# GpSimd in place of VectorE for the sums that rebuild a block of h

## The chip, the cores and the metric

The kernel runs on one core of one Trainium2 chip, in one launch, in fp32. The metric is the device time of a run in microseconds (us). The engines are TensorE (PE; its weight loads are PEld), VectorE (DVE), ScalarE (ACT), GpSimd (POOL) and SyncE (SP), which issues most of the DMAs. Each engine works through its own list of instructions in order, and they wait for each other by semaphores.

## The reference, cut to what matters

Two layers over 512 latent and 256 context tokens of width 1024. Each layer is a half feed-forward block, a token mixer, and another half feed-forward block, each modulated by adaLN and followed by a layer norm. The part that the change touches is the feed-forward block:

```python
def half_ffn(x, shift, scale, gate, w_in, w_out, g, b):
    h = modulate(x, shift, scale)
    a, u = jnp.split(h @ w_in, 2, axis=-1)
    y = (jax.nn.silu(a) * u) @ w_out
    return layernorm(ALPHA * x + 0.5 * gate * y, g, b)
```

It runs four times. Three of these calls are over all 768 tokens (`ffn0`, `ffn1` and `ffn2`, the "wide" ones); the last one, `ffn3`, is over the latent tokens alone and is built by other code.

## The kernel before, in words

**Precision.** Each fp32 operand of a product is split into a high part (a copy rounded to the matmul format fp32r) and a low part (the operand less its high part). A product is three matmuls: high by high, high by low, low by high. `HHI` and `HLO` hold the parts of h, 8 chunks of 128 rows by 768 tokens.

**Seven products.** A wide feed-forward block has 11 iterations (`FI`), each for two slots, A and B, of 128 columns of the gate half and of the value half. From iteration 2 on, the product of h with these columns is done by a seven-product scheme (`up`, L3153) on blocks of h: half of the rows by half of the tokens (`HALF` is 384). Four blocks are mixtures, kept as high parts `TH_` and low parts `TL_` (numbers 1, 2 and 3, each as two tiles k of 2 chunks by 384 tokens); the fourth mixture overwrites a quarter of h itself, the first four chunks over the last 384 tokens. The seven products of a slot come in this order: "11", "T2", "21", "T3", "T1", "T4", "22"; each is 12 matmuls of 384 columns. The semaphore `g_pe` counts the first five, `pe[slot]` the last two. Between them VectorE adds the results up in `P1`, `U3` and `GM` (`second_sum`, `gate_first`, `third_sum`, `fourth_sum`, `up_second`, `up_first`, `gate_second`), ScalarE applies silu to each half of `GM`, and VectorE multiplies (`gated_first`, `gated_second`).

**The last iteration** (L2326 to L2356 on VectorE, L3241 to L3245 on TensorE). Slot A goes through the seven products, then TensorE does the 16 groups of the previous iteration's second product (`down`, L3191), and slot B is done in the plain way (`up_classic` with `rebuilt`, L3094). `rebuilt` needs the quarter of h that was overwritten. So while the last slot A is in work, VectorE rebuilds it, for each k: `rebuild_mix(k)` sums high and low of block "11" and both parts of block 1 in the tile `TM_[2][k]`, three sums of 128x768 elements, each of which waits for the one before; `rebuild_parts(k)` splits that tile in `TH_[2][k]` (a copy) and `TL_[2][k]` (a difference). `TM_[2]` lies in the same bytes as `TL_[2]`, so it waits until product "T2" of this slot is done (`g_pe` at 5 * first + 2). `rebuild_mix(0)` stands between `gate_first` and `third_sum`; `rebuild_parts(0)` after `up_second`; `rebuild_mix(1)` between `gated_first` and `gate_second`; `rebuild_parts(1)` after the first four `accumulate`. In `ffn0` and `ffn1`, `tables()` (14 and 21 tiny VectorE instructions on coefficients) stands after `rebuild_parts(0)`.

**Banks.** `accumulate(i, e)` (L2043) adds the result e of `down` to X and so frees its PSUM bank. TensorE's groups e = 0 to 3 need no bank freed; group 4 waits until `accumulate` 0 is done (L3208).

**Other lines that are spoken of.** `split_lo` (L1719) makes the low part of a 128x1024 slab of weights, after ScalarE has made its high part (L1059). GpSimd (L802 on) issues the loads of the adaLN weights and makes partial sums for the layer norms (`add_chunks`, L838, first needed when X gets its last results); in the odd mixer it makes low parts too (L925, L959). L1837 centers X for a layer norm, L2267 adds the last results to X, L2771 scales a softmax row in the odd mixer.

Of the kernel before, what the change touches and what calls it, by code (L numbers as in the profile page):

```python
# [24 lines left out]
HALF = TOK // 2  # L25
# [6 lines left out]
FI = FC // 2  # L32
# [6 lines left out]
F32 = mybir.dt.float32  # L39
F32R = mybir.dt.float32r  # L40
ACT = mybir.ActivationFunctionType
ALU = mybir.AluOpType
# [105 lines left out]
def build(nc, A, out):  # L148
    stack = ExitStack()

    def sem(name):
        return nc.alloc_semaphore(name)
# [4 lines left out]
    def sb(name, shape, dt=F32, at=None):  # L157
        size = 4 * int(np.prod(shape[1:]))
        if at is None:
            at = free[0]  # L160
            free[0] += -(-size // 32) * 32
        assert at + size <= 229344, (name, at + size - 229344)
        return nc.alloc_sbuf_tensor_at(name, list(shape), dt, offset=at)
# [4 lines left out]
    HHI = sb("HHI", [P, KC, TOK], F32R)  # L168
    HLO = sb("HLO", [P, KC, TOK], F32R)
# [37 lines left out]
    def region(start, end):  # L207
# [3 lines left out]
        def place(name, shape, dt=F32):  # L211
# [13 lines left out]
    TH_ = {n: [place(f"TH{n}{k}", [P, 2, HALF], F32R) for k in range(2)] for n in (1, 2)}  # L225
    TL_ = {n: [place(f"TL{n}{k}", [P, 2, HALF], F32R) for k in range(2)] for n in (1, 2)}
    TL_[3] = [place("TL30", [P, 2, HALF], F32R)]
    TM_ = {n: [sb(f"TM{n}{k}", [P, 2, HALF], F32, at=r2 + 17408 + 3072 * (4 + 2 * (n - 1) + k)) for k in range(2)]
           for n in (1, 2)}
# [147 lines left out]
    s_pe, s_max, s_nb, s_exp, s_inv, s_norm, t_pe, pt_hi, pt_lo, av_pe, o_tmp, o_add = (  # L377
        sem(n) for n in ("s_pe", "s_max", "s_nb", "s_exp", "s_inv", "s_norm", "t_pe", "pt_hi", "pt_lo", "av_pe", "o_tmp", "o_add"))
    g_hi, g_lo, g_mix, g_pe, g_p1, g_add = (sem(f"seven_{n}") for n in ("hi", "lo", "mix", "pe", "p1", "add"))
    t_mix, t_hi, t_lo = (sem(f"t_{n}") for n in ("mix", "hi", "lo"))  # L380
    och_hi, och_lo = sem("och_hi"), sem("och_lo")
    fin_x, fin_tr, fin_cp = sem("fin_x"), sem("fin_tr"), sem("fin_cp")
    h_hi, h_lo = sem("h_hi"), sem("h_lo")
# [5 lines left out]
    count = dict(q=0, A=0, B=0, W=0, evac=0, g=0, gB=0, gs=0, ln=0, h=0, tr=0, ada=0, taken=0)  # L389
# [42 lines left out]
    def raw_slot(q):  # L432
        return q % 2
# [77 lines left out]
    BLOCKS = {"ffn0": 0, "ffn1": 1, "ffn2": 2}  # L511

    def wide_q(name, kind, i):

        q = plan[name].q
        if isinstance(i, int) and i == 0:
            return q + {"B": 2, "A": 4, "W0": 6}[kind]
        if isinstance(i, int) and i == FI - 1:
            return q + 6 * i + {"W1": 1, "B": 2, "W0": 4, "W1L": 5}[kind] - 6 * i
        return q + {"B": 1, "W1": 3, "A": 4, "W0": 6}[kind]  # L520

    def seven(name, slot, i):

        return UNITS * BLOCKS[name] + 2 * (i - 2) + "AB".index(slot)
# [21 lines left out]
    def last_evac(name, S, a, m):  # L546

        return plan[name].evac + KC * S * (FI - 1) + KC * a + m + 1
# [14 lines left out]
    def part(name, a):  # L563

        if name in HALVED:
            return CTX * a, CTX, 0
        s = ORDER[LN_PARTS[name]][a]
        return *SEGS[s], s
# [234 lines left out]
    def _(pool):  # L803
# [9 lines left out]
        def ada_loads(l, n0, group, i=0):  # L813

            for k in range(KC):
                slot = k % ADA_RING
                if not (isinstance(i, int) and KC * (n0 + i) + k < ADA_RING):

                    pool.wait_ge(ada_used, KC * n0 + k - ADA_RING + 1 + KC * i)
                src = A["ada_w"][l, k * P:(k + 1) * P, :].rearrange("p (g n) -> p g n", n=D)[  # L820
                    :, bass.ds(group, 1), :].squeeze(1)
                pool.dma_start(ADA[slot][:, :], src).then_inc(ada_in[slot], 16)  # L822
# [7 lines left out]
        def add_chunks(name, S, a, evicted):  # L830

            lo, n, _ = part(name, a)
            total, (count, done) = RSTD[:, lo:lo + n], adds(name, a)
            for m in range(1, count + 1):
                pool.wait_ge(evac, evicted(a, m))
                if m > 1:
                    pool.wait_ge(ln_add, done + m - 1)
                pool.tensor_tensor(total, X[:, 0, lo:lo + n] if m == 1 else total, X[:, m, lo:lo + n],  # L838
                                   ALU.add).then_inc(ln_add, 1)

        def last_sums(name, prev):

            evicted = lambda a, m: last_evac(prev, 2, a, m)
            add_chunks(name, 2, 0, evicted)
            add_chunks(name, 2, 1, evicted)

        last_sums("ln0", "ffn0")
        pool.wait_ge(evac, plan["ln0"].evac)
        for n in range(3):
# [19 lines left out]
        pool.wait_ge(evac, plan["ln1"].evac)  # L869
        with pool.Fori(0, N_ADA) as i:  # L870
            ada_loads(1, plan["ffn1"].ada, i, i)
        last_sums("ln2", "ffn1")
        last_sums("ln3", "ffn2")


# [117 lines left out]
    def _(act):  # L993
# [123 lines left out]
        def wide(name, ada, nxt):  # L1117
            p = plan[name]
            blk = BLOCKS[name]
# [80 lines left out]
                unit("B", i, lambda: rows_hi(1, wide_q(name, "W1", i), i, p.W + 2 * KC * (i - 1)), wide_q(name, "A", i))  # L1200

            def t_high(dst, src, count):
                act.wait_ge(t_mix, 28 * blk + count)
                act.activation(dst, src, ACT.Copy).then_inc(t_hi, 1)

            def blocks_hi(k):
# [20 lines left out]
            n, q = seven(name, "A", 2), wide_q(name, "A", 1)  # L1227
            first, second = RAW[raw_slot(q)], RAW[raw_slot(q + 1)]
# [29 lines left out]
            for e, s in enumerate(ORDER[2]):  # L1258
                lo, n = SEGS[s]
# [413 lines left out]
    def _(dve):  # L1673
# [20 lines left out]
        for n in range(2):  # L1694
            dve.wait_ge(f_pe, n + 1)
            for s in range(2):
                lo, w = SEGS[s]
# [315 lines left out]
        def wide(name, j, ada, t0, then, nxt, tables=None):  # L2013
            p = plan[name]
            blk = BLOCKS[name]
# [40 lines left out]
            def gate_first(slot, i):  # L2056

                dve.wait_ge(g_pe, 5 * seven(name, slot, i) + 3)
                dve.tensor_tensor(GM[slot][:, 0:HALF], PS[2 if slot == "A" else 5][:, 0:HALF], P1[:, :],
                                  ALU.add).then_inc(g_add, 1)  # L2060

            def third_sum(slot, i):

                v = seven(name, slot, i)
                dve.wait_ge(mul["BA"["AB".index(slot)]], p.gs + 2 * (i if slot == "A" else i + 1))
                dve.wait_ge(g_pe, 5 * v + 4)
                dve.wait_ge(g_add, 7 * v + 1)
                dve.tensor_tensor(U3[:, :], PS[0 if slot == "A" else 3][:, 0:HALF], GM[slot][:, HALF:TOK],
                                  ALU.add).then_inc(g_add, 1)
# [21 lines left out]
            def gated_first(slot, i):  # L2091
                dve.wait_ge(g_add, 7 * seven(name, slot, i) + 6)
                dve.wait_ge(silu[slot], p.gs + 2 * i + 1)
                dve.tensor_tensor(GM[slot][:, 0:HALF], GM[slot][:, 0:HALF], U3[:, :], ALU.mult).then_inc(mul[slot], 1)

            def gate_second(slot, i):

                dve.wait_ge(pe[slot], (p.A if slot == "A" else p.B) + 2 * i + 2)
                dve.tensor_tensor(GM[slot][:, HALF:TOK], PS[0 if slot == "A" else 3][:, 0:HALF], GM[slot][:, HALF:TOK],
                                  ALU.add).then_inc(g_add, 1)  # L2100
# [99 lines left out]
            def mixed(ins, count):  # L2200

                ins.then_inc(t_mix, 1)
                return 28 * blk + count

            def blocks_mixed(k):

# [13 lines left out]

            def blocks_low(k):

                dve.wait_ge(t_mix, 28 * blk + 6 * k + 6)
                for m, n in enumerate((1, 3, 2)):
                    dve.wait_ge(t_hi, 6 * blk + 3 * k + m + 1)
                    dve.tensor_tensor(TL_[n][k][:, :, :], TM_[n][k][:, :, :], TH_[n][k][:, :, :].bitcast(F32),
                                      ALU.subtract).then_inc(t_lo, 1)
# [12 lines left out]
                dve.wait_ge(t_mix, done)  # L2240
                dve.tensor_tensor(HLO[:, x, HALF:TOK], t, HHI[:, x, HALF:TOK].bitcast(F32), ALU.subtract).then_inc(t_lo, 1)  # L2241

            def rebuild_mix(k):

                x, t = slice(2 * k, 2 * k + 2), TM_[2][k][:, :, :]
                first = seven(name, "A", FI - 1)
                dve.wait_ge(g_pe, 5 * first + 2)
                done = mixed(dve.tensor_tensor(t, HHI[:, x, 0:HALF].bitcast(F32), HLO[:, x, 0:HALF].bitcast(F32), ALU.add),
                             20 + 4 * k + 1)
                dve.wait_ge(t_mix, done)  # L2250
                done = mixed(dve.tensor_tensor(t, t, TH_[1][k][:, :, :].bitcast(F32), ALU.add), 20 + 4 * k + 2)
                dve.wait_ge(t_mix, done)
                mixed(dve.tensor_tensor(t, t, TL_[1][k][:, :, :].bitcast(F32), ALU.add), 20 + 4 * k + 3)

            def rebuild_parts(k):

                t = TM_[2][k][:, :, :]
                dve.wait_ge(t_mix, 28 * blk + 20 + 4 * k + 3)
                done = mixed(dve.tensor_copy(TH_[2][k][:, :, :], t), 20 + 4 * k + 4)
                dve.wait_ge(t_mix, done)  # L2260
                dve.tensor_tensor(TL_[2][k][:, :, :], t, TH_[2][k][:, :, :].bitcast(F32), ALU.subtract).then_inc(t_lo, 1)

# [66 lines left out]
            second_sum("A", last)  # L2329
            split_lo("W", 0, p.q + 6 * last, 0)  # L2330
            gate_first("A", last)
            rebuild_mix(0)
            third_sum("A", last)
            split_lo("W", 1, wide_q(name, "W1", last), last)
            fourth_sum("A", last)
# [3 lines left out]
                tables()  # L2339
            up_first("A", last)  # L2340
            gated_first("A", last)
            rebuild_mix(1)
            gate_second("A", last)
            gated_second("A", last)
            q = wide_q(name, "B", last)
# [14 lines left out]
            for e, s in enumerate(ORDER[2]):  # L2360
                lo, n = SEGS[s]
# [424 lines left out]
        for a in range(2):  # L2786
            inverse("final", 1, a)
            lo, n, _ = part("final", a)
# [879 lines left out]
```

## Time and profile before

| | |
|---|---|
| median of 3 runs | 2967.43 us (2966.73 to 2968.1) |
| profiled execution, its own time | 2960.28 us |
| span of that execution | 2958.6 us |
| PE busy | 2870.8 us, 97% of the span |
| DVE busy | 2030.3 us, 69% |
| ACT busy | 1051.6 us, 36% |
| POOL busy | 294.6 us, 10% |
| mean granted clock of TensorE | 0.991 |

The span is the time from the first to the last instruction of the one profiled execution; its own time is 1.7 us more. Busy times leave out waits. A row of the timeline gives the start in us, the duration in us, the engine, the line, the operation, output<-inputs, the shape and the number of instructions merged in it (consecutive ones overlap a little, so that two in a row take less than two durations), and in square brackets the idle time before it with what ended it.

### The profile page before, as it was taken

The numbers are of one execution on the slowest core, as the hardware profiler recorded it, in microseconds if no ns is written. First come the engines' busy times: TensorE is split into PE (matmuls) and PEld (weight loads), VectorE is DVE, ScalarE is ACT, GpSimd is POOL, SyncE is SP. The second block draws the span as 40 slices with busy tenths as digits, with TensorE's granted clock in tenths as the row PEclk, the third lists the DMA queues.
The fourth block names the chain that finished last, engine by engine and source line by source line (L and its number), as shares of the span: only waits on it lengthen the run. The fifth ranks groups of instructions, "written<-read, shape, count | busy, mean of one in ns | idle before, by whom it ended". The sixth has DMA issues, their size and how long they took to land.

```text
span 2958.6 us, 44154 instructions
## 1 busy us (share of the span) xinstructions
PE 2870.8 (97%) x16175; PEld 2475.9 (84%) x16175; DVE 2030.3 (69%) x3250; ACT 1051.6 (36%) x1654; POOL 294.6 (10%) x403
## 2 busy tenths in 40 slices
PE   6999999999999999999999999999999999999998
PEld 2688999987875878998988889999878998878887
DVE  3467767777767477676776887777776887654545
ACT  1423323325650332232223433333255665422223
POOL 1000000001000100101001000000003654000000
PEclk8999999999999999999999999999999999999999
DMA  7444442221213233534432122222310101233331
GB/s 278 149 136 150 140 130 64 64 72 46 60 59 114 86 100 115 173 125 158 129 96 58 43 64 76 66 71 64 88 48 20 29 21 44 63 118 96 94 99 43
DMA packets 301697, 269.64 MB, mean 91 GB/s; under 512 B 31176, under 2 KB 257328, under 8 KB 301457
## 3 DMA queue, kind: packets, MB, share of 16 engines
q1 hardware_dynamic: 278960, 188.95, 21.4%
q0 software_dynamic: 21760, 76.03, 7.3%
q10 hardware_dynamic: 864, 3.15, 0.3%
q8 instruction: 72, 1.18, 0.2%
q14 instruction: 41, 0.33, 0.0%
HBM read 262.85 MB, written 5.24 MB: 91 GB/s over the span
## 4 chain that ended last, share of the span: by engine, by line
PE 87%; DVE 6%; DMA 2%; ACT 2%; issue 1%; POOL 1%; SPq 0%; POOLq 0%; DVEq 0%; ACTq 0%
PE PSALL L2905 14%; PE PSALL L2906 14%; PE PSALL L2907 14%; PE PSALL L3148 8%; PE PSALL L3149 8%; PE PSALL L3150 8%; PE PSALL L2812 2%; PE PSALL L2951 2%; PE PSALL L2927 2%; PE PSALL L2952 2%; PE PSALL L2953 2%; PE PSALL L3571 1%; PE PSALL L3556 1%; PE PSALL L2854 1%; DMA RAW<-in_ffn_w_in_dram 1%
## 5 line engine op out<-in xcount | busy, mean ns | idle before, releaser
L2043 DVE SCALAR_TENSOR_TENSOR X<-PSALL,GATE,X 128x512 f32<-128x512 f32 x480 | 279.5, 611 | 102.7 <-PE PSALL L2907 102.1
L3148 PE MATMUL PSALL<-HHI,WSH 128*128 128x384 f32 x816 | 273.7, 335 | 5.5 <-DVE HLO L2241 5.5
L3149 PE MATMUL PSALL<-HLO,WSH 128*128 128x384 f32 x816 | 273.2, 335 | 0.0
L3150 PE MATMUL PSALL<-HHI,WSL 128*128 128x384 f32 x816 | 273.1, 335 | 0.0
L2905 PE MATMUL PSALL<-GHIA,WHIW 128*128 128x512 f32 (+1 forms) x624 | 219.4, 352 | 16.7 <-DVE X L2043 11.1
L2906 PE MATMUL PSALL<-GLOA,WHIW 128*128 128x512 f32 (+1 forms) x624 | 215.0, 345 | 0.0
L2907 PE MATMUL PSALL<-GHIA,WLOW 128*128 128x512 f32 (+1 forms) x624 | 214.6, 344 | 0.0
L2905 PE MATMUL PSALL<-GHIB,WHIW 128*128 128x512 f32 (+1 forms) x624 | 214.2, 343 | 0.0
L2907 PE MATMUL PSALL<-GHIB,WLOW 128*128 128x512 f32 (+1 forms) x624 | 214.0, 343 | 0.0
L2906 PE MATMUL PSALL<-GLOB,WHIW 128*128 128x512 f32 (+1 forms) x624 | 213.9, 343 | 0.0
L1168 ACT ACTIVATE WSH<-RAW 128x512 fp32r<-128x512 f32 x204 | 129.1, 633 | 224.0 <-DVE RAW L2120 151.2
L3148 PE MATMUL PSALL<-TH,WSH 128*128 128x384 f32 x612 | 208.6, 341 | 0.0
L3149 PE MATMUL PSALL<-TL,WSH 128*128 128x384 f32 x612 | 207.6, 339 | 0.0
L3150 PE MATMUL PSALL<-TH,WSL 128*128 128x384 f32 x612 | 207.5, 339 | 0.0
L2905 PE MATMUL PSALL<-HHI,WHIA 128*128 128x512 f32 (+1 forms) x464 | 168.9, 364 | 1.5 <-DVE WLOA L1719 1.5
L2907 PE MATMUL PSALL<-HHI,WLOA 128*128 128x512 f32 (+1 forms) x464 | 165.3, 356 | 0.0
L2906 PE MATMUL PSALL<-HLO,WHIA 128*128 128x512 f32 (+1 forms) x464 | 165.3, 356 | 0.0
L1059 ACT ACTIVATE WHIW<-RAW 128x1024 fp32r<-128x1024 f32 x96 | 100.1, 1055 | 178.3 <-PE PSALL L2907 94.7
L822 POOL DMA_DIRECT2D ADA<-in_ada_w_dram x144 | 76.3, 530 | 829.6 <-PE PSALL L2812 735.5
L2905 PE MATMUL PSALL<-HHI,WHIB 128*128 128x512 f32 (+1 forms) x432 | 157.5, 365 | 1.3 <-DVE MOD L1709 1.3
L3148 PEld LDWEIGHTS PSALL<-HHI,WSH 128*128 128x128 f32 x816 | 153.4, 188 | 6.4 <-issue 6.4
L838 POOL TENSOR_TENSOR RSTD<-X 128x256 f32<-128x256 f32 (+1 forms) x12 | 13.2, 1099 | 1423.1 <-DVE X L2267 875.1
(396 smaller groups left out, 7325.5 us busy)
## 6 DMA issues: line engine op xcount, KB each, us to landing
RAW<-in_ffn_w_in_dram SPq DMA_DIRECT2D x176, 512.0 KB, 4.1
ADA<-in_ada_w_dram POOLq DMA_DIRECT2D x144, 512.0 KB, 5.7
RAW<-in_ffn_w_out_dram SPq DMA_DIRECT2D x88, 512.0 KB, 3.9
RAW<-in_ev_w_in_dram SPq DMA_DIRECT2D x20, 512.0 KB, 4.1
WRAW<-in_mla_w_q_up_dram SPq DMA_DIRECT2D x16, 288.0 KB, 3.0
RAW<-in_ev_w_out_dram SPq DMA_DIRECT2D x8, 512.0 KB, 4.6
RAW<-in_mla_w_in_dram SPq DMA_DIRECT2D x8, 512.0 KB, 4.4
RAW<-in_mla_w_out_dram SPq DMA_DIRECT2D x8, 512.0 KB, 4.0
```

Of the source, the lines that this page charges most:

```text
L822: pool.dma_start(ADA[slot][:, :], src).then_inc(ada_in[slot], 16)
L1059: act.activation(WHI[slot][:, 1024 * half:1024 * half + 1024], RAW[raw_slot(q)][:, :], ACT.Copy).then_inc(hi_done, 1)
L1168: return act.activation(WSH[:, place, :], raw[:, 512 * cols:512 * cols + 512], ACT.Copy)
L2043: dve.scalar_tensor_tensor(X[:, m, lo:lo + n], down_bank(m, s, 2), GATE[:, j, m, s:s + 1], X[:, m, lo:lo + n], ALU.mult, ALU.add).then_inc ...
L2812: x = te.matmul(PS[3][32 * j:32 * j + 32, 0:D // 4], SC[:, k, :], ADA[slot][:, j * D // 4:(j + 1) * D // 4], start=(k == 0), stop=(k == KC ...
L2905: te.matmul(out, w_hi, x_hi(k), start=(k == 0), stop=False)
L2906: te.matmul(out, w_hi, x_lo(k), start=False, stop=False)
L2907: x = te.matmul(out, w_lo, x_hi(k), start=False, stop=(k == ks - 1))
L2927: x = te.matmul(stat_bank(name, a), ONES[:, :], squares_at(name, a, m), start=(m == 0), stop=(m == KC - 1))
L3148: te.matmul(out, w_hi, hi[block](k), start=(k == 0), stop=False)
L3149: te.matmul(out, w_hi, low[block](k), start=False, stop=False)
L3150: x = te.matmul(out, w_lo, hi[block](k), start=False, stop=(k == 3))
```

## The change

The three sums for k = 0 and k = 1 leave VectorE's list. GpSimd gets them as `block_again(name, k)`, in one piece for both k, ahead of the layer-norm sums that follow the block. It waits for the same product "T2" and counts each sum in a semaphore of its own, `t_again`; each sum waits for the one before it. `rebuild_parts(k)` stays on VectorE at its place, and waits for `t_again`. The counts of `t_mix` are adapted.

```diff
@@ -377,7 +377,7 @@
     s_pe, s_max, s_nb, s_exp, s_inv, s_norm, t_pe, pt_hi, pt_lo, av_pe, o_tmp, o_add = (
         sem(n) for n in ("s_pe", "s_max", "s_nb", "s_exp", "s_inv", "s_norm", "t_pe", "pt_hi", "pt_lo", "av_pe", "o_tmp", "o_add"))
     g_hi, g_lo, g_mix, g_pe, g_p1, g_add = (sem(f"seven_{n}") for n in ("hi", "lo", "mix", "pe", "p1", "add"))
-    t_mix, t_hi, t_lo = (sem(f"t_{n}") for n in ("mix", "hi", "lo"))
+    t_mix, t_hi, t_lo, t_again = (sem(f"t_{n}") for n in ("mix", "hi", "lo", "again"))
     och_hi, och_lo = sem("och_hi"), sem("och_lo")
     fin_x, fin_tr, fin_cp = sem("fin_x"), sem("fin_tr"), sem("fin_cp")
     h_hi, h_lo = sem("h_hi"), sem("h_lo")
@@ -844,6 +844,21 @@
             add_chunks(name, 2, 0, evicted)
             add_chunks(name, 2, 1, evicted)
 
+        def block_again(name, k):
+
+            x, t = slice(2 * k, 2 * k + 2), TM_[2][k][:, :, :]
+            blk = BLOCKS[name]
+            done = 6 * blk + 3 * k
+            pool.wait_ge(t_lo, 10 * blk + 8)
+            pool.wait_ge(g_pe, 5 * seven(name, "A", FI - 1) + 2)
+            pool.tensor_tensor(t, HHI[:, x, 0:HALF].bitcast(F32), HLO[:, x, 0:HALF].bitcast(F32), ALU.add).then_inc(t_again, 1)
+            pool.wait_ge(t_again, done + 1)
+            pool.tensor_tensor(t, t, TH_[1][k][:, :, :].bitcast(F32), ALU.add).then_inc(t_again, 1)
+            pool.wait_ge(t_again, done + 2)
+            pool.tensor_tensor(t, t, TL_[1][k][:, :, :].bitcast(F32), ALU.add).then_inc(t_again, 1)
+
+        for k in range(2):
+            block_again("ffn0", k)
         last_sums("ln0", "ffn0")
         pool.wait_ge(evac, plan["ln0"].evac)
         for n in range(3):
@@ -869,7 +884,11 @@
         pool.wait_ge(evac, plan["ln1"].evac)
         with pool.Fori(0, N_ADA) as i:
             ada_loads(1, plan["ffn1"].ada, i, i)
+        for k in range(2):
+            block_again("ffn1", k)
         last_sums("ln2", "ffn1")
+        for k in range(2):
+            block_again("ffn2", k)
         last_sums("ln3", "ffn2")
 
 
@@ -1200,7 +1219,7 @@
                 unit("B", i, lambda: rows_hi(1, wide_q(name, "W1", i), i, p.W + 2 * KC * (i - 1)), wide_q(name, "A", i))
 
             def t_high(dst, src, count):
-                act.wait_ge(t_mix, 28 * blk + count)
+                act.wait_ge(t_mix, 22 * blk + count)
                 act.activation(dst, src, ACT.Copy).then_inc(t_hi, 1)
 
             def blocks_hi(k):
@@ -2200,7 +2219,7 @@
             def mixed(ins, count):
 
                 ins.then_inc(t_mix, 1)
-                return 28 * blk + count
+                return 22 * blk + count
 
             def blocks_mixed(k):
 
@@ -2220,7 +2239,7 @@
 
             def blocks_low(k):
 
-                dve.wait_ge(t_mix, 28 * blk + 6 * k + 6)
+                dve.wait_ge(t_mix, 22 * blk + 6 * k + 6)
                 for m, n in enumerate((1, 3, 2)):
                     dve.wait_ge(t_hi, 6 * blk + 3 * k + m + 1)
                     dve.tensor_tensor(TL_[n][k][:, :, :], TM_[n][k][:, :, :], TH_[n][k][:, :, :].bitcast(F32),
@@ -2240,23 +2259,11 @@
                 dve.wait_ge(t_mix, done)
                 dve.tensor_tensor(HLO[:, x, HALF:TOK], t, HHI[:, x, HALF:TOK].bitcast(F32), ALU.subtract).then_inc(t_lo, 1)
 
-            def rebuild_mix(k):
-
-                x, t = slice(2 * k, 2 * k + 2), TM_[2][k][:, :, :]
-                first = seven(name, "A", FI - 1)
-                dve.wait_ge(g_pe, 5 * first + 2)
-                done = mixed(dve.tensor_tensor(t, HHI[:, x, 0:HALF].bitcast(F32), HLO[:, x, 0:HALF].bitcast(F32), ALU.add),
-                             20 + 4 * k + 1)
-                dve.wait_ge(t_mix, done)
-                done = mixed(dve.tensor_tensor(t, t, TH_[1][k][:, :, :].bitcast(F32), ALU.add), 20 + 4 * k + 2)
-                dve.wait_ge(t_mix, done)
-                mixed(dve.tensor_tensor(t, t, TL_[1][k][:, :, :].bitcast(F32), ALU.add), 20 + 4 * k + 3)
-
             def rebuild_parts(k):
 
                 t = TM_[2][k][:, :, :]
-                dve.wait_ge(t_mix, 28 * blk + 20 + 4 * k + 3)
-                done = mixed(dve.tensor_copy(TH_[2][k][:, :, :], t), 20 + 4 * k + 4)
+                dve.wait_ge(t_again, 6 * blk + 3 * k + 3)
+                done = mixed(dve.tensor_copy(TH_[2][k][:, :, :], t), 20 + k + 1)
                 dve.wait_ge(t_mix, done)
                 dve.tensor_tensor(TL_[2][k][:, :, :], t, TH_[2][k][:, :, :].bitcast(F32), ALU.subtract).then_inc(t_lo, 1)
 
@@ -2329,7 +2336,6 @@
             second_sum("A", last)
             split_lo("W", 0, p.q + 6 * last, 0)
             gate_first("A", last)
-            rebuild_mix(0)
             third_sum("A", last)
             split_lo("W", 1, wide_q(name, "W1", last), last)
             fourth_sum("A", last)
@@ -2339,7 +2345,6 @@
                 tables()
             up_first("A", last)
             gated_first("A", last)
-            rebuild_mix(1)
             gate_second("A", last)
             gated_second("A", last)
             q = wide_q(name, "B", last)
```

## Rows read from the trace of the kernel before

**Rows 1.** The page: busy time, share of the span, instructions.
```profile
PE 2870.8 (97%) x16175; PEld 2475.9 (84%) x16175; DVE 2030.3 (69%) x3250; ACT 1051.6 (36%) x1654; POOL 294.6 (10%) x403
```
**Rows 2.** The page: chain that ended last, its share by engine.
```profile
PE 87%; DVE 6%; DMA 2%; ACT 2%; issue 1%; POOL 1%; SPq 0%; POOLq 0%; DVEq 0%; ACTq 0%
```
**Rows 3.** Timeline, PE: group 4 of `down` in the last iteration, three blocks.
```profile
617.73 0.80 PE L2905 MATMUL PSALL<-GHIA,WHIW 128*128 128x512 f32 x1 [2.84 <-DVE X L2043]
...
1552.27 0.50 PE L2905 MATMUL PSALL<-GHIA,WHIW 128*128 128x512 f32 x1 [3.65 <-DVE X L2043]
...
2097.82 0.50 PE L2905 MATMUL PSALL<-GHIA,WHIW 128*128 128x512 f32 x1 [1.09 <-DVE X L2043]
```
**Rows 4.** Chain that ended last, 600 to 640 us: start, us, engine, line.
```profile
612.55 0.88 DVE TM L2248
...
617.01 0.67 DVE X L2043
```
**Rows 5.** Timeline, DVE, last slot A of ffn0.
```profile
600.35 0.56 DVE L2053 TENSOR_TENSOR GMA<-PSALL,P 128x384 f32<-128x384 f32 x1 [1.54 <-PE PSALL L3150]
600.82 1.22 DVE L1719 TENSOR_TENSOR WLOW<-RAW,WHIW 128x1024 fp32r<-128x1024 f32 x1
...
606.12 1.22 DVE L1719 TENSOR_TENSOR WLOW<-RAW,WHIW 128x1024 fp32r<-128x1024 f32 x1
...
608.19 0.55 DVE L2259 CAST TH<-TM 128x768 fp32r<-128x768 f32 x1
608.77 0.96 DVE L2261 TENSOR_TENSOR TL<-TM,TH 128x768 fp32r<-128x768 f32 x1
...
611.99 0.56 DVE L2094 TENSOR_TENSOR GMA<-GMA,U 128x384 f32<-128x384 f32 x1
...
616.46 0.56 DVE L2104 TENSOR_TENSOR GMA<-GMA,P 128x384 f32<-128x384 f32 x1 [0.59 <-ACT GMA L1152]
```
**Rows 6.** Timeline, ACT, the same stretch.
```profile
603.36 1.05 ACT L1059 ACTIVATE WHIW<-RAW 128x1024 fp32r<-128x1024 f32 x1
```
**Rows 7.** Groups of POOL's instructions by shape: busy us, mean ns.
```profile
L925 POOL TENSOR_TENSOR KL<-K,KH 64x768 fp32r<-64x768 f32 x16 | 29.5, 1844 | 43.4 <-ACT KH L1553 43.4
...
L959 POOL TENSOR_TENSOR WLOA<-RAW,WHIA 128x1024 fp32r<-128x1024 f32 x2 | 4.7, 2362 | 1.2 <-ACT WHIA L1059 1.2
```
**Rows 8.** Timeline, POOL and DVE at once, after ffn0.
```profile
662.30 1.85 DVE L1837 TENSOR_TENSOR X<-X,MU 128x256 f32<-128x256 f32 x2
662.46 1.41 POOL L838 TENSOR_TENSOR RSTD<-X 128x512 f32<-128x512 f32 x1 [3.81 <-DVE X L2267]
...
664.74 2.05 DVE L2267 SCALAR_TENSOR_TENSOR X<-PSALL,GATE,X 128x512 f32<-128x512 f32 x3
665.56 1.28 POOL L838 TENSOR_TENSOR RSTD<-RSTD,X 128x512 f32<-128x512 f32 x1 [1.70 <-DVE X L2267]
666.72 3.43 DVE L1719 TENSOR_TENSOR WLOB<-RAW,WHIB 128x1024 fp32r<-128x1024 f32 x2
666.98 2.09 POOL L838 TENSOR_TENSOR RSTD<-RSTD,X 128x512 f32<-128x512 f32 x1
```
**Rows 9.** Timeline, POOL and DVE at once, in the odd mixer.
```profile
2478.88 4.68 POOL L959 TENSOR_TENSOR WLOA<-RAW,WHIA 128x1024 fp32r<-128x1024 f32 x2 [1.20 <-ACT WHIA L1059]
2481.50 2.49 DVE L2771 TENSOR_SCALAR PR<-PR,STAT 128x768 f32<-128x768 f32 x1
```
**Rows 10.** Single lines over the whole trace: ns min/median/max.
```profile
L1837 DVE TENSOR_TENSOR X<-X,MU x96: 406/418/1517, 660.3 to 2937.8; 128x256 f32<-128x256 f32 x64, 128x512 f32<-128x512 f32 x32
...
L1719 DVE TENSOR_TENSOR WLOB<-RAW,WHIB x56: 1207/1218/2298, 126.6 to 2887.2; 128x1024 fp32r<-128x1024 f32 x56
...
L2771 DVE TENSOR_SCALAR PR<-PR,STAT x64: 619/620/2487, 2263.0 to 2498.3; 128x768 f32<-128x768 f32 x64
```
**Rows 11.** Windows: us, PE, PEld, DVE, ACT, POOL busy, granted clock, DMA.
```profile
619.00:621.00 2.00, 2.00 (x6) 1.52 (x6) 1.84 (x4) 0.00 (x0) 0.00 (x0) 0.51 0.00 0
...
2097.80:2100.00 2.20, 2.18 (x9) 1.80 (x10) 2.17 (x5) 0.61 (x1) 0.00 (x0) 1.00 0.00 0
```

## The prediction

> **What bounds the kernel now.** I read the page first: PE is busy for 97% of the span and VectorE for 69% [rows 1], and 87% of the chain that ended last is PE, 6% VectorE [rows 2]. So a VectorE instruction taken away is worth something only where PE waits for VectorE. Then I read PE's waits in the three stretches that the change touches. Each holds one wait that matters, at the same place: group 4 of `down` in the last iteration needs a bank that VectorE's first `accumulate` frees. It costs 2.84, 3.65 and 1.09 us in ffn0, ffn1 and ffn2 [rows 3], 7.58 us in all. The chain of waits shows whose time it is: the second trio of sums, `rebuild_mix(1)`, from 612.55 on, stands in it, and the first `accumulate` at 617.01 releases PE [rows 4]. The first trio lies behind PE's products, which VectorE follows closely. The three stalls differ by the tiny table instructions: in ffn0 14 of them and `up_first` fill the time from the end of L2261 (609.73) to L2094 (611.99) [rows 5]; ffn1 has 21, ffn2 none.
>
> Read alone, this promises nearly the whole 7.58 us. The catch is in GpSimd's rows.
>
> **What is removed, added and moved, per block.** VectorE loses six sums of 128x768 elements, 0.95 to 0.96 us each. GpSimd gains six. It does nothing else there, and its next work is the layer-norm sums after 650 us, so no queue is disturbed; no DMA is issued or moved. The new wait stands before the copy in `rebuild_parts`; behind it on VectorE queue the tables, `up_first`, `gated_first` and with them the bank that PE waits for.
>
> **What a sum costs on GpSimd.** No row shows 128x768. 128x512 takes 1.28 us undisturbed [rows 8], 128x1024 2.36 [rows 7]; the middle is 1.82, and 16 instructions of 64x768 took a mean of 1.84 [rows 7]. I take 1.84, and about 0.14 us from the end of one to the start of the next that waits for it (between the two L838 at 665.56 and 666.98: 1.42 less 1.28). Bounds: 1.7, if the flat shape helps, and 2.1.
>
> **What the two engines do to each other.** At 662.46 GpSimd starts a sum of 1.41 us, and two L1837 of VectorE take 1.85 us together, where one alone takes 0.42: one of them was held until GpSimd was done [rows 8, 10]. At 666.98 GpSimd's sum takes 2.09 instead of 1.28, because it is held by the L1719 that VectorE had begun; the second L1719, next in VectorE's list, is then held in turn: 3.43 us for two that take 1.22 each [rows 8, 10]. So the two take turns, and the one that comes second waits for the whole instruction of the first. The three L2267 beside the sum at 665.56, with one input in PSUM, take 2.05 us, as three in a row do without it, and so go by freely [rows 8]. A one-input instruction in SBUF is not free: L2771 takes 2.49 us instead of 0.62 beside a GpSimd sum of 128x1024 [rows 9, 10]. The copy of `rebuild_parts` is such a one (0.55 us for 768 elements, against 0.96 for a sum of the same size [rows 5]).
>
> The Trainium skill says the same in "SBUF — State Buffer", section "Who interferes with whom": VectorE's second pair of SBUF ports is GpSimd's only one, and whoever issues second is blocked for the whole instruction, if VectorE has two SBUF inputs or runs a copy in its two-port mode. By this rule the six moved sums still cost VectorE time, and the trace agrees (the 1.41 and 2.09 us sums above). The skill's "GPSIMD Engine Reference", section 3.1, gives 4497 ns for a sum of 2048 elements; scaled to 768 that is an estimate of 1.69 us, by which the sum below would be 2 us instead of 4.5.
>
> **The walk through ffn0.** I laid the instructions out in order with these durations. In VectorE's list a lone one takes its row's time, a following one starts 0.08 us before the end of the last, and a held one ends one streaming time after GpSimd's end (1.08 us for L1719: 3.43 less what the first took). The same walk without the change puts the end of the first `accumulate` at 617.65; it was 617.68 [rows 4].
> - 600.35: "T2" is done [rows 5]. GpSimd's sum 1 runs to 602.19. The L1719 of 600.82 is held, and ends at 603.27 instead of 602.04.
> - Sum 2 is ready at 602.33, held by that L1719 until 603.13, ends 604.97. Sum 3: 605.11 to 606.95.
> - The second L1719 has its high half at 605.30 (the silu and L1059 on ScalarE follow `gate_first`, which has moved to 603.2; L1059 takes 1.05 [rows 6]). Sum 3 is 0.2 us ahead of it: held, it ends at 608.02, against 607.34 before [rows 5]. All that removing the first trio could give is lost here.
> - Sum 4 (k = 1) was held by it: 607.88 to 609.72. The copy comes at 608.87 and is held: 610.13. Sum 5: 609.99 to 611.83; the difference is held: 612.64 (before: 609.73 [rows 5]). Sum 6: 612.50 to 614.34; the first table instruction is held until then.
> - Now VectorE is alone: the other 13 table instructions to 615.90, `up_first`, `gated_first` to 617.08, `gate_second` 617.54, silu with its 0.59 us wait and `gated_second` [rows 5] 618.70, first `accumulate` 619.36.
>
> So GpSimd's six sums end 14 us after "T2" (6 x 1.84, 0.56 of gaps, 2.4 held by VectorE), and everything that PE waits for comes after them. Against 617.65 that is 1.71 us later; the stall grows from 2.84 to 4.5 us. ffn1 is the same with longer tables: 1.71. In ffn2 `up_first` (an input in PSUM) goes by during sum 6 and only `gated_first` is held, until 614.34 on ffn0's scale: 1.12 us later. `rebuild_parts(1)` finds its sums done. Behind the stall PE and VectorE go on as before, so all of it reaches the end: 1.71 + 1.71 + 1.12 = **4.54 us**. On the profiled execution's own time of 2960.28 that is 2964.8. The median of the runs is 7.15 us above that execution, by something no row shows; I add the sum to the median: 2967.43 + 4.54 = **2972.0**.
>
> Bounds by the same walk: with sums of 1.7 us 0.87 + 0.87 + 0.28 = 2.0; with 2.1 us 3.35 + 3.35 + 2.76 = 9.5. If the copy is not held: 1.9.
>
> **TensorE's clock.** After the stall of 2.84 us the granted clock is 0.51 from 619 to 621 us, the lower of its two levels (1.2 GHz) [rows 11]; the seven matmuls there cost 0.2 us more each, some 1.5 us. After ffn2's 1.09 us it stays at 1.00 [rows 11]. Longer stalls in ffn0 and ffn1 don't add to what is lost already, as more of the slow stretch is spent waiting; a stall of 2.2 us in ffn2 could bring it there too, 1.5 us.
>
> **Rivals.**
> - *The full gain* (the other side). If GpSimd's sums did not hold VectorE, the first `accumulate` would end at 614.14 on ffn0's scale, before PE needs it: 2.84 + 3.51 + 1.09 = 7.4 us, and the slow clock after the two long stalls goes with them, 3: 2957. It decides at the second L1719 and the copy: if both take their lone times, this is the case. For it: VectorE has room for it and it is what the chain of waits suggests. Against: every overlap of such instructions in the trace [rows 8, 9].
> - *Slower sums.* If a sum takes 2.1 us (the first one reads strided halves of two tensors), or GpSimd starts 0.5 us late, or the clock falls in ffn2: 1.5 to 5 us on top, 2973.5 to 2977. For it: the walk gives some 6 us for each us that a sum takes longer. Against: the shapes of rows 7 lie close together.
> - *A partial hold.* If the copy and the small table instructions slip through between sums, or sums take 1.7 us: +2 us, 2969.5.
>
> **Chances.** Forecast as walked 0.50, partial hold 0.17, slower sums or clock 0.23, full gain 0.10. A measurement of this kernel tells about 0.2% (5.9 us) from no change. Faster by more: 0.10, all from the full gain. Slower by more, above 2973.4: the last rival but its low end, and a third of the forecast's own spread (2969 to 2975): 0.36. Between: 0.54. The range of 8 in 10 leaves out the full gain and the far end of the slower sums: 2965 to 2978.
>
> **What the changed profile would show.** Right: GpSimd's six sums some 14 us long in each block with gaps or lengthened members; an L1719 and the L2261 at about twice their time or more; PE's wait at group 4 at 4.5, 5.3 and 2.2 us. Wrong: VectorE's instructions there at their lone times and that wait gone (full gain), or GpSimd's sums well away from 1.84 us where nothing holds them. The prediction also fails if VectorE, not GpSimd, wins the turns, so that the sums end late but PE's bank does not.

## The result, and the profile after

| | before | changed |
|---|---|---|
| median of 20 runs each | 2963.41 us | 2968.03 us |
| ratio, 95% interval | | 1.0017 (1.001 to 1.0024) |
| profiled execution, span | 2958.6 us | 2965.2 us |
| POOL busy | 294.6 us | 335.2 us |
| DVE busy | 2030.3 us | 2033.6 us |
| PE's waits for L2043 (L2062 after) in ffn0, ffn1, ffn2 | 2.84, 3.65, 1.09 us | 4.54, 5.34, 2.20 us |

The kernel is 0.17% slower, 5.0 us by the ratio. (The three runs of before that were shown ahead of the prediction had a median of 2967.43 us; over 20 it is 4.0 us lower.) VectorE has lost 18 sums of some 0.95 us, 17 us of work, and yet its busy time has grown by 3.3 us: what holds an instruction up counts as its duration.

The timeline of PE shows group 4 of `down`; the line numbers of the changed kernel are 5 higher on PE and 19 higher on the `accumulate` of VectorE. These answer to [rows 3], each one longer:

```profile
619.01 0.79 PE L2910 MATMUL PSALL<-GHIA,WHIW 128*128 128x512 f32 x1 [4.54 <-DVE X L2062]
...
1555.10 0.79 PE L2910 MATMUL PSALL<-GHIA,WHIW 128*128 128x512 f32 x1 [5.34 <-DVE X L2062]
...
2103.71 0.50 PE L2910 MATMUL PSALL<-GHIA,WHIW 128*128 128x512 f32 x1 [2.20 <-DVE X L2062]
```

GpSimd's timeline in ffn0, the six moved sums:

```profile
599.95 1.84 POOL L854 TENSOR_TENSOR TM<-HHI,HLO 128x768 f32<-128x768 f32 x1 [183.20 <-PE PSALL L3155]
601.88 2.71 POOL L856 TENSOR_TENSOR TM<-TM,TH 128x768 f32<-128x768 f32 x1
604.66 1.85 POOL L858 TENSOR_TENSOR TM<-TM,TL 128x768 f32<-128x768 f32 x1
606.47 2.83 POOL L854 TENSOR_TENSOR TM<-HHI,HLO 128x768 f32<-128x768 f32 x1
609.37 2.04 POOL L856 TENSOR_TENSOR TM<-TM,TH 128x768 f32<-128x768 f32 x1
611.49 2.43 POOL L858 TENSOR_TENSOR TM<-TM,TL 128x768 f32<-128x768 f32 x1
```

Two of the six take 1.84 and 1.85 us; the other four are longer by the time for which VectorE holds them. This is VectorE beside them, which answers to [rows 5]:

```profile
600.40 2.47 DVE L1738 TENSOR_TENSOR WLOW<-RAW,WHIW 128x1024 fp32r<-128x1024 f32 x1
...
604.89 2.70 DVE L1738 TENSOR_TENSOR WLOW<-RAW,WHIW 128x1024 fp32r<-128x1024 f32 x1 [0.24 <-ACT WHIW L1078]
...
608.44 1.27 DVE L2266 CAST TH<-TM 128x768 fp32r<-128x768 f32 x1
609.75 2.48 DVE L2268 TENSOR_TENSOR TL<-TM,TH 128x768 fp32r<-128x768 f32 x1
612.15 1.80 DVE L1817 TENSOR_SCALAR CG<-MOD 128x16 f32<-128x16 f32 x1
```

Read the two fences against each other. The first L1738 comes during GpSimd's first sum, which ends at 601.79, and ends 1.08 us after it, at 602.87. The second comes 0.2 us after the third sum has begun; that sum ends at 606.51, and the L1738 again 1.08 us later. The copy ends 0.4 us after the fourth sum, the difference 0.8 us after the fifth. A table instruction on 16 elements, which takes 0.17 us alone, takes 1.80 behind the sixth.

The windows show the granted clock (the column ahead of the last two), which answers to [rows 11]. The lower level, 0.50, holds to 624 us; in the kernel before, the window from 621 to 624 us is at 1.00.

```profile
619.00:621.00 2.00, 1.99 (x5) 1.60 (x6) 1.97 (x5) 0.60 (x1) 0.00 (x0) 0.50 0.00 0
621.00:624.00 3.00, 3.00 (x9) 2.32 (x8) 1.61 (x2) 0.00 (x0) 0.00 (x0) 0.50 0.00 0
```

### The profile page after: what moved, and what is told of

The parts are those of the page before. It is cut to its first block, busy times and chain, and to the rows that moved or that the text cites. A ratio compares the mean times of both kernels' runs of the same rounds, so it can differ in the third digit from the quotient of the medians.

```text
span 2965.2 us, 44160 instructions
## 1 busy us (share of the span) xinstructions
PE 2872.7 (97%) x16175; PEld 2480.0 (84%) x16175; DVE 2033.6 (69%) x3232; ACT 1051.0 (35%) x1654; POOL 335.2 (11%) x421
## 4 chain that ended last, share of the span: by engine, by line
PE 88%; DVE 6%; DMA 2%; ACT 2%; issue 1%; POOL 1%; SPq 0%; POOLq 0%; DVEq 0%; ACTq 0%
PE PSALL L2910 14%; PE PSALL L2911 14%; PE PSALL L2912 14%; PE PSALL L3153 8%; PE PSALL L3154 8%; PE PSALL L3155 8%; PE PSALL L2817 2%; PE PSALL L2956 2%; PE PSALL L2932 2%; PE PSALL L2957 2%; PE PSALL L2958 2%; PE PSALL L3576 2%; PE PSALL L3561 1%; PE PSALL L2859 1%; DMA RAW<-in_ffn_w_in_dram 1%
## 5 line engine op out<-in xcount | busy, mean ns | idle before, releaser
L2062 DVE SCALAR_TENSOR_TENSOR X<-PSALL,GATE,X 128x512 f32<-128x512 f32 x480 | 279.6, 611 | 104.4 <-PE PSALL L2912 103.9
L2911 PE MATMUL PSALL<-HLO,WHIB 128*128 128x512 f32 (+1 forms) x432 | 154.6, 358 | 0.0
```

The lines of the kernel that those rows point to most:

```text
L2062: dve.scalar_tensor_tensor(X[:, m, lo:lo + n], down_bank(m, s, 2), GATE[:, j, m, s:s + 1], X[:, m, lo:lo + n], ALU.mult, ALU.add).then_inc ...
L2911: te.matmul(out, w_hi, x_lo(k), start=False, stop=False)
```

## The experiments

Ratios are to the kernel before, with 95% intervals. The diffs are cut to the lines that matter, without the counts of semaphores; what stands behind `#` in them was added to say where a line stands. "By turns" in the expectations is the reading that VectorE and GpSimd take turns, each waiting for the whole instruction of the other; PE's waits are those at group 4 of `down`, in the order ffn0, ffn1, ffn2.

**e1_writes_only.** Does GpSimd's work hold VectorE because it reads SBUF, or because it is there?

```diff
-            pool.tensor_tensor(t, HHI[...], HLO[...], ALU.add).then_inc(t_again, 1)
...
+            for n in range(6):
+                if n:
+                    pool.wait_ge(t_again, done + n)
+                pool.memset(t, 0.0).then_inc(t_again, 1)
```

> The changed kernel with each of GpSimd's sums replaced by two memsets of the same tile (the sums, and with them the rebuilt quarter of h, are left out of the computation). GpSimd is busy in about the same stretch (twelve memsets of some 0.75 us and gaps, 10 to 11 us after product T2) and VectorE waits for it by the same semaphore, but GpSimd reads no SBUF. Theory (VectorE's two-input instructions and GpSimd's reads take turns at one thing): the two L1738 (split_lo) take their lone 1.22 us, L2268 0.96, PE's wait at group 4 is 0 to 1 us in each block, and the kernel is 7 to 11 us faster than before (ratio 0.9965). Rival (anything GpSimd does in SBUF holds VectorE): L1738 and L2268 are lengthened by 0.4 to 0.7 us each, PE's waits stay at 2 us or more in ffn0, ratio 0.999 to 1.001. The copy L2266 may be held by a memset in both (up to 1.3 us), which would show that copies are held by writes as well.

Measured: 0.9965 (0.9955 to 0.9976). PE's waits are 0.25, 1.05 and none. GpSimd is at work for 9.7 us in a row, and VectorE's three two-input instructions in SBUF take their lone times:

```profile
598.23 9.71 POOL L857 MEMSET TM<- 128x768 f32 x12 [183.17 <-PE PSALL L3154]
```

```profile
598.71 1.22 DVE L1737 TENSOR_TENSOR WLOW<-RAW,WHIW 128x1024 fp32r<-128x1024 f32 x1
...
602.87 1.22 DVE L1737 TENSOR_TENSOR WLOW<-RAW,WHIW 128x1024 fp32r<-128x1024 f32 x1
...
605.40 1.05 DVE L2265 CAST TH<-TM 128x768 fp32r<-128x768 f32 x1
606.49 0.96 DVE L2267 TENSOR_TENSOR TL<-TM,TH 128x768 fp32r<-128x768 f32 x1
607.37 0.60 DVE L1816 TENSOR_SCALAR CG<-MOD 128x16 f32<-128x16 f32 x1
```

The copy (0.55 alone) and the one-input table instruction (0.17 alone) are still held, by the writes. So here two-input instructions of VectorE meet only GpSimd's reads, and one-input ones meet its writes too. A memset is also shorter than a sum (0.74 us against 1.84), but that is not why the two-input instructions go free, since the same memsets hold the copy. That handing the work over costs next to nothing in itself is shown as well: VectorE waits for the same semaphore here, and its busy time is 15.4 us less than in the kernel before. In e1 and e2 the rebuilt quarter of h is zero; whether that alters the time elsewhere was not tested, but the waits and the lone times are read from the trace and don't rest on it.

**e2_one_write.** What the six sums are worth, wherever they are done: one memset for each k in place of three sums.

```diff
-            pool.tensor_tensor(t, HHI[...], HLO[...], ALU.add).then_inc(t_again, 1)
...
+            pool.memset(t, 0.0).then_inc(t_again, 3)
```

> The changed kernel with GpSimd's three sums per k replaced by one memset (the sums are left out of the computation). What the sums are worth wherever they are done: the walk puts the first accumulate at 614.14 on the scale of ffn0 before, so PE's wait at group 4 is 0, 0.1 and 0 us in ffn0, ffn1, ffn2, and no slow clock follows it. 7.4 us of waiting and about 3 us of slow clock less than before: ratio 0.9965. The rival that the time is lost elsewhere in the stage (TensorE's own order, weights that come late) would leave a wait of over 1 us somewhere between the last slot A and slot B.

Measured: 0.9969 (0.9958 to 0.998), and no wait of PE for VectorE is left in the last iterations. By the ratios of e2 and e1, 9 and 10 us are to be had (their intervals reach from 6 to 13 us). The waits are 7.6 us of that in e2 and 6.3 in e1.

**e3_k0_only and e4_k1_only.** One half of the change each.

```diff
 e3:
+            rebuild_mix(1)      # VectorE, between gated_first and gate_second
-            block_again("ffn0", 1)
 e4:
+            rebuild_mix(0)      # VectorE, between gate_first and third_sum
-            block_again("ffn0", 0)
```

> GpSimd makes the sums of k = 0 only; those of k = 1 are back on VectorE at their old place. By turns: only three GpSimd sums (600.3 to 606.9 on ffn0's scale), the two L1738 are held (2.5 and 2.7 us), the copy and L2268 are not (0.55, 0.96); PE's waits at group 4: 3.4, 4.2, 1.7 us, so +0.6 us per block against before, 1.8 us in all, ratio 1.0006. Rival (VectorE is relieved by three sums, 2.85 us, and GpSimd is merely slow): waits of 1.4, 2.2 and 0, and a kernel 3 to 5 us faster than before.

Measured: 1.0016 (1.0006 to 1.0026); waits 3.50, 4.30 and 1.75 us:

```profile
622.23 0.79 PE L2927 MATMUL PSALL<-GHIA,WHIW 128*128 128x512 f32 x1 [3.50 <-DVE X L2062]
...
2103.42 0.63 PE L2927 MATMUL PSALL<-GHIA,WHIW 128*128 128x512 f32 x1 [1.75 <-DVE X L2062]
```

The waits that the walk gave are right within 0.1 us. Their sum is 2.0 us longer than before, and the interval of the time, 1.8 to 7.7 us, just holds that. Part of the rest is the clock, which in this execution fell after ffn2's wait as well (0.50 from 2104 to 2106 us, and the 0.63 of the last row against 0.50 in [rows 3]).

> GpSimd makes the sums of k = 1 only, from product T2 on; those of k = 0 are back on VectorE at their old place. GpSimd's sums now meet L1738 and the three sums of k = 0 on VectorE. By turns: VectorE's first trio takes some 4 us more for the turns, which removing the second trio (2.85 us) just does not pay; PE's waits 3.5, 4.3, 1.75 us, +0.65 us per block against before, ratio 1.0007. Rival (the critical trio, the one in the chain of waits, is gone from VectorE, and the early one had slack): waits 0, 0.8, 0 us, ratio 0.9970.

Measured: 1.0012 (1.0002 to 1.0021). Slower, as by turns, but the wait has split, which I had not foreseen, and its sum is smaller than forecast, 8.9 us against 9.55: VectorE's first trio takes 5.6 us (2.13, 2.48 and 0.96 where 0.95, 0.96 and 0.96 are its lone times), so that `third_sum` is late for the product "22", and only the rest shows at group 4.

```profile
605.55 2.13 DVE L2271 TENSOR_TENSOR TM<-HHI,HLO 128x768 f32<-128x768 f32 x1
607.72 2.48 DVE L2271 TENSOR_TENSOR TM<-TM,TH 128x768 f32<-128x768 f32 x1
```

```profile
611.71 0.44 PE L3170 MATMUL PSALL<-HHI,WSH 128*128 128x384 f32 x1 [1.23 <-DVE U L2087]
...
620.33 0.80 PE L2927 MATMUL PSALL<-GHIA,WHIW 128*128 128x512 f32 x1 [2.04 <-DVE X L2062]
```

In ffn0 that is 3.27 us in all, 4.08 and 1.52 in the others. Taking away the trio that stands in the chain of waits [rows 4] did not help as long as its replacement met VectorE's other work.

**e5_k1_late and e6_k0_dve_k1_late.** GpSimd makes the sums of k = 1 only after `gated_second`; `rebuild_parts(1)` stands after `accumulate` 11. In e6 the sums of k = 0 are back on VectorE at their old place.

```diff
+            if late:
+                pool.wait_ge(mul["A"], plan[name].gs + 2 * FI)
...
-            rebuild_parts(1)                    # after accumulate 3
+            rebuild_parts(1)                    # after accumulate 11
 e6 only:
+            rebuild_mix(0)                      # VectorE, between gate_first and third_sum
```

> Both k on GpSimd as in the changed kernel, but the sums of k = 1 start only when gated_second of the last slot A is done, and rebuild_parts(1) stands after accumulate 11. By turns: three GpSimd sums instead of six lie ahead of the first accumulate; the accumulates read PSUM and go by the others freely. PE's waits at group 4: 0.6, 1.4, 0 us; against before 5.6 us of waiting and some slow clock less: ratio 0.9975. Rival (the sums of k = 0 alone already cost what the change costs, since the loss arises at the two L1738): waits above 3 us in ffn0, ratio 1.0005 or more.

Measured: 0.9967 (0.9956 to 0.9977); waits 0.65, 1.46 and none.

> k = 0 on VectorE at its old place, k = 1 on GpSimd, started when gated_second is done, rebuild_parts(1) after accumulate 11. Nothing meets on the way to the first accumulate: waits 0, 0.8, 0 us, 6.8 us of waiting and about 3 us of slow clock less than before: ratio 0.9967. If rebuild_parts(1) or the split of slot B's weights comes too late, a new wait of PE shows in slot B.

Measured: 0.997 (0.9958 to 0.9982); waits none, 0.80 and none. GpSimd's three sums now lie beside `accumulate`, which has an input in PSUM. Neither holds the other: four `accumulate` take the 2.19 us that they take without GpSimd, and the sums 1.84 and 1.85. What is held is one split of weights later (2.52 us instead of 1.22), for which PE does not wait.

```profile
613.85 1.85 POOL L857 TENSOR_TENSOR TM<-HHI,HLO 128x768 f32<-128x768 f32 x1 [197.18 <-DVE GMA L2123]
615.77 1.84 POOL L859 TENSOR_TENSOR TM<-TM,TH 128x768 f32<-128x768 f32 x1
617.70 1.85 POOL L861 TENSOR_TENSOR TM<-TM,TL 128x768 f32<-128x768 f32 x1
```

```profile
613.58 2.19 DVE L2062 SCALAR_TENSOR_TENSOR X<-PSALL,GATE,X 128x512 f32<-128x512 f32 x4
...
618.11 2.52 DVE L1738 TENSOR_TENSOR WLOB<-RAW,WHIB 128x1024 fp32r<-128x1024 f32 x1
```

**e7_dve_late.** About the same place, but VectorE does it: all six sums on VectorE, those of k = 1 one by one between the accumulates, 4 to 10 us later after "T2" than in the kernel before.

```diff
             for e in range(4):
                 accumulate(last - 1, e)
+            rebuild_sum(1, 0)
             for e in range(4, 6):
                 accumulate(last - 1, e)
...
+            rebuild_sum(1, 1)           # after accumulate 7
+            rebuild_sum(1, 2)           # after accumulate 11
+            rebuild_parts(1)            # after accumulate 13
```

> All six sums on VectorE; those of k = 1 one by one between the accumulates after the first four, rebuild_parts(1) after accumulate 13. If the place and not the engine is what counts, this gives as much as e6: waits 0, 0.8, 0 us at group 4, ratio 0.9967. VectorE has some 2 us to spare for each four accumulates, and gets 4.3 us more to do in twelve; a wait of PE of up to 1 us later in down or at slot B would be the price, ratio then 0.9975.

Measured: 0.996 (0.9945 to 0.9975), a median of 2951.08 us against 2964.36 for the kernel before beside it, 11.9 us less by the ratio. Waits none, 0.81 and none; no later one appears. It is the lowest ratio, but with six runs its interval overlaps those of e5 and e6: that VectorE does it as well as GpSimd is shown, that it does it better is not.

**e8_tables_late.** e6 with `tables()` behind the first four accumulates.

```diff
             rebuild_parts(0)
-            if tables is not None:
-                tables()
...
                 accumulate(last - 1, e)          # e = 0 to 3
+            if tables is not None:
+                tables()
```

> As e6, with tables() after the first four accumulates instead of ahead of up_first. It takes the last 0.8 us of wait from ffn1: waits 0, 0, 0 us at group 4; ratio 0.9964 against before, 0.8 us faster than e6 if nothing behind it gets late. The tables' 1.7 and 2.6 us now stand ahead of accumulate 4, where they meet GpSimd's sums of k = 1: if the small table instructions are held by these, one by one, PE waits 1 to 3 us at groups 8 and later in ffn0 and ffn1, and e8 is slower than e6.

Measured: 0.9973 (0.9964 to 0.9981). The wait at group 4 is gone in ffn1, but 1.36 and 2.18 us appear at group 8 in ffn0 and ffn1. So the gain that was expected did not come, and the price that the expectation named did. In each of the two blocks two small instructions of the tables are held by GpSimd, for 0.5 and 1.5 us, one of them for most of a sum. Those 2.1 us are more than the whole wait in ffn0, and all but 0.1 us of it in ffn1. The rows of ffn0:

```profile
618.51 0.70 DVE L1817 TENSOR_SCALAR CG<-MOD 128x16 f32<-128x16 f32 x1
...
619.46 1.70 DVE L1821 TENSOR_TENSOR CB<-CB,MOD 128x16 f32<-128x16 f32 x1
```

Whether e8 is slower than e6, the two ratios (0.9973 and 0.997) don't tell.

## Why the prediction was right

*The bound.* Right: the three waits of [rows 3] grew by 1.70, 1.69 and 1.11 us. Of PE's other waits for VectorE none grew by more than 0.2 us; one shrank by 0.6 and one of 0.7 is gone. e2 shows no other wait behind these three in the last iterations: without the sums they are gone, and the granted clock stays at 1.00.

*The cost of a sum on GpSimd.* Taken as 1.84 us from 64x768 and the middle of two widths; measured 1.83 to 1.85 where nothing holds it, which puts the lower bound of 1.7 and the estimate of 1.69 out. The gap between dependent sums is 0.07 to 0.09 us, not 0.14.

*The turns.* The walk gave GpSimd's six sums 14.0 us from "T2" on; they took 14.0 (599.95 to 613.92). Within that, the gaps were 0.3 us where the walk had 0.56, and VectorE held the sums for 2.7 us where it had 2.4. The two misses cancel, and not by luck alone: a sum that is ready earlier is held for longer, until the same end. The walk gave the two L1719 (now L1738) ends at 2.9 and 7.7 us after "T2", measured 2.9 and 7.6. In ffn2 `up_first` went by in 0.54 us and `gated_first` was held, 1.62 us instead of 0.56, as walked. Predicted waits 4.5, 5.3 and 2.2; measured 4.54, 5.34 and 2.20. Their sum grew by 4.50 us against 4.54 forecast. That it is the reads that hold the two-input instructions was only argued then; e1 shows it.

*The clock.* I wrote that longer stalls in ffn0 and ffn1 add nothing to what the slow clock costs. That was wrong in this execution. In ffn0 the lower level lasted until 624 us instead of 621, and PE worked 5 us in it instead of 3.3, which cost some 0.9 us more. In ffn1 PE worked 4.1 us in it instead of 3.3, some 0.4 us more. It did not fall in ffn2. That makes 5.8 of the 6.6 us between the two spans (an estimate from the waits and the windows); the rest lies in other stages, which the change does not touch. There the clock differs between the two executions: behind the same wait of 3.21 us early in ffn2 it was 0.50 for the next 4 us in the changed kernel and 1.00 before. So a wait of this length does not decide by itself whether it falls, and e3, whose longer waits of 3.50 and 4.30 us were followed by no longer a slow stretch than before, shows that the extra cost need not come. The ratio of 20 runs, 5.0 us with 3 to 7 in its interval, does not tell 4.5 from 5.8.

*The rivals.* The full gain does not come as long as the sums read while VectorE reads: e1 and e6 show what it would have been, waits of 0 to 1 us. The partial hold is out, since the copy (1.27 us) and the small table instruction (1.80) were held. Slower sums did not happen. The predicted 2972.0 lies 4.0 us above the measured median, as much as the three runs of before lay above its median over 20; the change itself, 4.54 us forecast, measured 5.0.

What I left unsaid is the better place: the trio of k = 1 was needed on neither engine before the first `accumulate` (e6, e7).

## What to carry to other kernels

Before work is given to GpSimd, lay its instructions beside VectorE's and mark those that read two tensors in SBUF, or copy or scale within it: each of them can wait for a whole GpSimd instruction, and GpSimd for it, so that work moved off VectorE may cost it more than it frees. Put such work where VectorE has an input in PSUM, as e6 does. And ask first whether it must be on the way to the awaited result at all: moving one trio 4 to 10 us down VectorE's own list gained 0.4%, moving it to GpSimd at that later place 0.3%, and moving both trios to GpSimd at the early place lost 0.17%.

## What the runs showed of the hardware that was not expected

Memsets on GpSimd leave two-input instructions of VectorE at their lone 1.22 and 0.96 us, but lengthen a copy (0.55 to 1.05) and a one-input instruction of 16 elements (0.17 to 0.60). The expectation of e1 had left the copy open. A small instruction is held like a large one, and not only a one-input one: on 16 elements, L1817 with one input took 1.80 us in the changed kernel and L1821 with two took 1.70 in e8, where each takes 0.17 alone.
